# Sixty-four weighted rows of a hosted gather moved from VectorE to diagonal products on TensorE, with six diagonals instead of four

## What is computed

```python
def block(args):
    xt, it, gt = args
    act = jax.nn.gelu(jnp.einsum('td,tkd->tk', xt, peer_u[it]), approximate=False)
    return jnp.einsum('tk,tkd->td', gt * act, peer_v[it])
```

## Time and profile before

| | |
|---|---|
| median of 3 runs | 2608.33 us (2603.61 to 2612.64) |
| profiled execution | 2615.07 us, its span 2613.3 us |
| mean granted TensorE clock | 0.927 |
| TensorE busy, matmuls | 2158.4 us, 83% |
| VectorE busy | 1646.6 us, 63% |
| ScalarE busy | 1003.3 us, 38% |
| GpSimd busy | 697.2 us, 27% |
| products L2452 | 900.2 us busy |
| dots L2406 | 617.5 us busy |
| folds L2415 | 82.0 us busy |

### The profile page before, as it was taken

One profiled execution on the slowest core, in us unless ns is written; L12 is line 12 of the kernel. 1 busy time (PEld: TensorE's weight loads), 2 busy tenths in 40 slices (PEclk: granted clock), 3 DMA queues, 4 the chain that ended last, 5 costly groups with the idle time before them and its releaser, 6 DMA issues. The chain is left out here.

```text
span 2613.3 us, 25560 instructions
## 1 busy us (share of the span) xinstructions
PE 2158.4 (83%) x8090; PEld 1338.1 (51%) x8090; DVE 1646.6 (63%) x3385; ACT 1003.3 (38%) x2477; POOL 697.2 (27%) x606
## 2 busy tenths in 40 slices
PE   6999978898788687777868887676777797899998
PEld 5778855676323232322324453232334474788877
DVE  5674266535788988878457776665766655655534
ACT  3213346323343333333334344435533455433322
POOL 0120021000444454443435444444444100000000
PEclk9999988998899999998989999888988797999999
DMA  7663200211799999999999999999999533222222
GB/s 237 217 210 113 70 5 26 71 67 75 309 421 421 408 389 421 405 421 382 422 373 413 416 416 412 422 374 355 421 420 421 169 93 115 97 96 96 80 81 97
DMA packets 142827, 683.18 MB, mean 261 GB/s; under 512 B 19648, under 2 KB 36320, under 8 KB 74224
## 3 DMA queue, kind: packets, MB, share of 16 engines
q0 software_dynamic: 73728, 536.90, 50.1%
q1 hardware_dynamic: 68976, 144.78, 16.8%
HBM read 679.50 MB, written 2.10 MB: 261 GB/s over the span
## 5 line engine op out<-in xcount | busy, mean ns | idle before, releaser
L2452 PE MATMUL peer_Y<-peer_w,peer_diag 128*128 128x512 f32 x1784 | 900.2, 644 | 239.8 <-ACT peer_diag L2438 212.2
L2397 POOL DMA_INDIRECT peer_w<-in_peer_uv,peer_eidx x510 | 602.4, 1181 | 713.8 <-PE peer_Y L2452 464.2
L2406 DVE CUSTOM_DVE_ANT_0 peer_w<-peer_w,peer_xtok 128x1024 f32<-128x1024 f32 x510 | 617.5, 1222 | 198.4 <-DMA peer_w<-in_peer_uv,peer_eidx 195.7
L2452 PEld LDWEIGHTS peer_Y<-peer_w,peer_diag 128*128 128x128 f32 x1784 | 338.3, 202 | 750.0 <-ACT peer_diag L2438 441.5
L2430 ACT ACTIVATE peer_gel<-peer_dots 128x1 f32<-128x1 f32 x512 | 103.8, 203 | 721.3 <-DVE peer_dots L2406 721.0
L2438 ACT ACTIVATE peer_diag<-all_ident,peer_a 128x128 f32<-128x128 f32 x448 | 179.9, 402 | 17.9 <-PE peer_Y L2452 3.4
L2432 ACT ACTIVATE peer_a<-peer_gel,peer_gates 128x1 f32<-128x1 f32 x512 | 150.7, 294 | 16.6
L2961 PE MATMUL m_acc<-m2x_hs,m2x_cut 128*128 128x512 f32 (+1 forms) x384 | 143.7, 374 | 6.4 <-PEq L123 3.7
L2963 PE MATMUL m_acc<-m2x_hs,m2x_cut 128*128 128x512 f32 (+1 forms) x384 | 143.3, 373 | 0.0
L2962 PE MATMUL m_acc<-m2x_hs,m2x_cut 128*128 128x512 f32 (+1 forms) x384 | 143.2, 373 | 0.0
L1292 ACT ACTIVATE p_cut<-m1h_raw 128x512 fp32r<-128x512 f32 (+2 forms) x96 | 58.2, 609 | 203.6 <-PE p_acc L1239 121.0
(11 more groups left out here) (514 smaller groups left out, 3740.1 us busy)
## 6 DMA issues: line engine op xcount, KB each, us to landing
m_gates<-in_w_ada SPq DMA_DIRECT2D x48, 512.0 KB, 4.4
m2x_raw<-in_w_up SPq DMA_DIRECT2D x22, 1024.0 KB, 4.8
m1h_raw<-in_w_in SPq DMA_DIRECT2D x80, 256.0 KB, 3.0
m20h_raw<-in_w_in SPq DMA_DIRECT2D x48, 256.0 KB, 7.3
m22h_raw<-in_w_in SPq DMA_DIRECT2D x48, 256.0 KB, 2.8
m_down_ring<-in_w_down SPq DMA_DIRECT2D x22, 512.0 KB, 3.5
m_out_ring<-in_w_out SPq DMA_DIRECT2D x16, 512.0 KB, 7.8
peer_w<-in_peer_uv,peer_eidx POOLq DMA_INDIRECT x510, 16.7
```

What stands on the lines that cost most here:

```text
L2397: pool.indirect_dma_start(self.slot(n).rearrange("p c n -> p (c n)"), None, self.uv_dram, bass.IndirectOffsetOnAxis(self.col(self.eidx, n) ...
L2406: dve.tensor_tensor_reduce(u, u, self.xtok[:, n // PICKS, :], 1.0, 0.0, ALU.mult, ALU.add, self.col(self.dots, n)).then_inc(self.dotted, 1)
L2452: ins = pe.matmul(self.Y[:, h, :], self.diag[:, i % self.RD, :], self.slot(n)[:, 1, h * BANK:(h + 1) * BANK], start=(k == 0), stop=(i == l ...
```

## The change

No row is folded any more, so all 512 rows are products, and the ring of diagonal matrices has six places instead of four (1 KB more of each partition).

```diff
 class Gather:
 
 
-    RW, RD = 9, 4
+    RW, RD = 9, 6
     LOW, FIRST = 2, 4
-    FOLDED = range(2 * PICKS, NT * PICKS)
+    FOLDED = range(0)
     SHARE = 4
```

## The result

The changed kernel takes 2616.85 us (median of 20 executions, 2610.87 to 2622.00), the kernel before 2609.73 in the same measurement (20 executions, 2603.61 to 2615.63). The ratio is 1.0027, 95% interval 1.0019 to 1.0035: slower by 7.1 us, between 5.0 and 9.1. The forecast was +9.0 and 2617.4. The difference lies just inside the 0.3% that the prediction called no change, but the 95% interval does not hold 0. The profiled execution took 2618.64 us at a mean granted clock of 0.943 (before 0.927).

What follows compares the result with a forecast made beforehand. Transfers were taken to bound project and out, the host's chain the other stages. Norm +1, project 0, GLA +3.9, attention's start -2.5, end +3.2 and +3.4 sum to +9.0 on 2608.33: 2617.4 us, 8-in-10 range 2600 to 2632.

Runs made afterwards that it cites:

- the early gain: Kernel before with the norm's 4 KB gain loaded ahead of the gather instead of at the norm stage's start: 2604.60 us against 2610.99, ratio 0.9979.

## What to carry to other kernels

Before moving work from one engine to another inside a hosted loop, ask which engine the host waits for next: here TensorE was the busier one (2158 us against 1647) and stood in front of VectorE, so 76 us taken from the one cost 7 us on the other. Where transfers were full and TensorE had room, in project, the move was free, so each stage needs its own answer. At a stall, ask which engine's release opens the ring again behind it, and what else is in flight in it. And look first for the waits in which nothing is computed: the load of one table, issued a stage earlier, gained 8.4 us, where moving 64 rows lost 7.1.

## What was not expected of the hardware

- A table behind a stream of gathered rows takes long: the bias table, 1024 KB, needed 11.7 to 16.1 us from issue to landing at attention's start, and 25.5 to 26.7 when issued during GLA. The norm's gain, 4 KB, took 5.6.
- In project the granted clock was 0.96 before (TensorE busy for 202.35 of 241 us) and 0.99 to 1.00 with the folds as products (227.35 of 240). Over the whole program TensorE's busy time rose by 71.5 us for products that at 1.72 each make 110: the busy time of an engine whose clock moves doesn't add up.
- The start of the hosted half (the addition of tile 2) varied between 1326 and 1335 us over the profiled executions, whose earlier work differs in the ring and the early gain alone: more than the whole effect.
